# A half-block weight ring, reordered first casts and a moved lambda polynomial in a decoder layer

## What is computed

```
xn = rms_norm(x, mix_norm)
rnn_x, rnn_y, q, k_cmp, v_cmp, ..., merge_g = split(xn @ w_in)
y_rnn = gelu(rnn_y) * rg_lru(conv4(rnn_x), ..., rg_lambda)
y_nsa = native_sparse_attention(rms(q), compress_blocks(k_cmp, v_cmp; cmp_w1), ...)
y_sc  = sc_b * conv3(sc_c * sc_h)
x = x + (sum_b sigmoid(merge_g[b]) * (y_b @ P_b)) @ w_out
x = x + hierarchical_moe(rms_norm(x))      # 32 experts of 1024 x 256, top 1 group, top 2 in it
```

## Time and profile before

| | us |
|---|---|
| median of three runs | 462.19 |
| their lowest and highest | 461.26, 464.12 |
| profiled execution, span from first to last instruction | 459.2 |
| TensorE busy in it | 413.9 (90%) |
| VectorE busy | 217.9 (47%) |
| ScalarE busy | 173.8 (38%) |

### The profile page before, as it was taken

One profiled execution on the slowest core, in us unless ns is written; L12 is line 12 of the kernel. 1 busy time (PEld: TensorE's weight loads), 2 busy tenths in 40 slices (PEclk: granted clock), 3 DMA queues, 4 the chain that ended last, 5 costly groups with the idle time before them and its releaser, 6 DMA issues.

```text
span 459.2 us, 6635 instructions
## 1 busy us (share of the span) xinstructions
PE 413.9 (90%) x2701; PEld 292.7 (64%) x2701; DVE 217.9 (47%) x336; ACT 173.8 (38%) x270; POOL 40.0 (9%) x66
## 2 busy tenths in 40 slices
PE   6999999999999999999999999999929659299586
PEld 3889999999878787888888853535512413225122
DVE  5658988487799994564584650211100201002011
ACT  6558429873764565344256331110201101002001
POOL 8420490000000000000003100000000000000000
PEclk9999999999999999999999899999968959889799
DMA  8997893254552578897589989999999999999996
GB/s 291 348 260 257 327 387 105 100 184 184 183 183 93 185 250 298 286 410 266 183 364 359 387 355 425 423 421 420 428 424 421 422 422 425 424 414 414 400 394 220
DMA packets 43613, 146.27 MB, mean 319 GB/s; under 512 B 2908, under 2 KB 6097, under 8 KB 34242
## 3 DMA queue, kind: packets, MB, share of 16 engines
q1 hardware_dynamic: 42272, 143.50, 81.0%
q10 hardware_dynamic: 562, 1.84, 1.1%
q0 software_dynamic: 752, 0.55, 0.5%
HBM read 144.83 MB, written 1.05 MB: 318 GB/s over the span
## 4 chain that ended last, share of the span: by engine, by line
PE 62%; SPq 15%; DMA 14%; DVE 5%; ACT 2%; issue 2%; DVEq 0%
PE psum L1634 17%; DMA ring<-in_exp_w_down 10%; PE psum L1630 10%; PE psum L1877 7%; SPq L413 6%; PE psum L1927 5%; SPq L461 3%; PE psum L2145 3%; PE psum L2048 3%; DMA a_att<-in_exp_w_down 3%; SPq L429 3%; PE psum L1695 2%; SPq L418 2%; PE psum L2017 2%; PE psum L1769 1%
## 5 line engine op out<-in xcount | busy, mean ns | idle before, releaser
L1085 DVE TENSOR_TENSOR wl<-ring,wh 128x2048 fp32r<-128x2048 f32 (+1 forms) x38 | 85.1, 2245 | 36.5 <-ACT wh L750 35.8
L750 ACT CAST wh<-ring 128x2048 fp32r<-128x2048 f32 (+1 forms) x37 | 69.1, 1868 | 52.6 <-PE psum L1634 21.0
L1574 DVE COPY mix<-psum 128x512 f32<-128x512 f32 (+1 forms) x8 | 5.3, 658 | 115.7 <-PE psum L2145 110.0
L1634 PE MATMUL psum<-wh,x_parts 128*128 128x512 f32 (+1 forms) x256 | 58.1, 379 | 0.2 <-ACT a_att L877 0.2
L1634 PEld LDWEIGHTS psum<-wh,x_parts 128*128 128x128 f32 x256 | 46.0, 188 | 9.1 <-issue 0.4
L1035 ACT COPY mix<-psum 128x512 f32<-128x512 f32 x8 | 4.7, 586 | 103.5 <-PE psum L2145 100.4
L2048 PE MATMUL psum<-a_att,mix 128*32 128x512 f32 x96 | 25.6, 693 | 18.0 <-DMA a_rnn<-in_exp_w_up 17.0
L1630 PE MATMUL psum<-x_parts,wh 128*128 128x256 f32 x320 | 40.5, 284 | 0.0
L1630 PEld LDWEIGHTS psum<-x_parts,wh 128*128 128x128 f32 x320 | 39.1, 192 | 0.1
L2048 PE MATMUL psum<-odd,mix 128*32 128x512 f32 x192 | 24.2, 661 | 10.0 <-DMA odd<-in_exp_w_up 8.8
L2145 PE MATMUL psum<-ring,a_moe 128*32 128x512 f32 x152 | 27.6, 658 | 5.1 <-DMA ring<-in_exp_w_down 5.1
(11 more groups left out here) (319 smaller groups left out, 629.7 us busy)
## 6 DMA issues: line engine op xcount, KB each, us to landing
ring<-in_w_in SPq DMA_DIRECT2D x11, 2048.0 KB, 7.8
ring<-in_exp_w_down SPq DMA_DIRECT2D x19, 1024.0 KB, 15.8
odd<-in_exp_w_gate SPq DMA_DIRECT2D x12, 1024.0 KB, 14.8
odd<-in_exp_w_up SPq DMA_DIRECT2D x12, 1024.0 KB, 16.8
a_att<-in_exp_w_gate SPq DMA_DIRECT2D x8, 1024.0 KB, 14.9
a_att<-in_exp_w_up SPq DMA_DIRECT2D x8, 1024.0 KB, 16.9
mix<-in_exp_w_down SPq DMA_DIRECT2D x6, 1024.0 KB, 27.6
a_rnn<-in_exp_w_gate SPq DMA_DIRECT2D x4, 1024.0 KB, 21.4
```

The source lines that it names most:

```text
L750: a.copy(high, src).then_inc(hi_ready, 1)
L1085: signal(v.tensor_tensor(low, src, halves(m, wh)[1].bitcast(fp32), ALU.subtract), lo_ready, m + 1)
L1634: ins = t_.matmul(bank(name)[:, 0:n], xp[hf][:, k, i * P:(i + 1) * P], wv[:, k, :], start=start, stop=stop)
```

## The change

The ring has the same bytes, but the pieces now use only its upper half: three places of 2048 columns (1 MB), at column 6144. Piece m goes to place m mod 3. Each piece is loaded by its own DMA (piece 0 by two), and SP waits before piece m until `lo_ready` is m - 2, so until the low part of piece m - 3 is made. The lower half of the ring is free for other data: `cmp_w1` is loaded at once to columns 0 to 4095, right behind the first three pieces, and the same columns take `first_group(3)` as soon as the compression product is through. `down_half(0, 0)` goes to the columns behind, at once too. `odd_half(3, 0)` and `down_half(1, 0)` are issued behind pieces 3 and 4 instead of ahead of block sc. `even[3]` to `even[5]` are now the ring from the bottom up, and so the last three down halves change places. On ScalarE the two casts of q's piece 0 stand ahead of the upper halves of the input, and xT2 ahead of xT1. On VectorE the low part of piece 0 stands ahead of xT1 and xT3. The lambda chain stands between the low parts of pieces 4 and 5 instead of behind both.

```diff
-LOADS = (["q", "kva", "kvb", "rx", "cmp", "ry", "sb", "sc", "sh"]
+LOADS = (["q", "kva", "kvb", "rx", "ry", "sb", "sc", "sh"]
...
-        ring = sb("ring", [P, RING, SLOT])
+        ring = sb("ring", [P, 3 * SLOT])
+        HALF = SLOT // 2
+        PIECES_AT = 3 * SLOT - RING * HALF
+        cmp_weights = ring[:, 0:SLOT]
...
-                ring[:, 2, :], ring[:, 0, :], ring[:, 1, :]]
+                ring[:, 0:SLOT], ring[:, SLOT:2 * SLOT], ring[:, 2 * SLOT:]]
...
+        def piece_at(m):
+            return ring[:, PIECES_AT + (m % RING) * HALF:][:, 0:HALF]
...
+            def load_piece(m):
+
+                if m >= RING:
+                    sp.wait_ge(lo_ready, m - RING + 1)
+                name, hf = PIECES[m]
+                dst = halves(m, wh)[0]
+                if m == 0:
+                    for i in range(2):
+                        k = slice(2 * i, 2 * i + 2)
+                        sp.dma_start(dst[:, k], piece_source(name, hf)[:, k]).then_inc(q_quarter[i], 16)
+                else:
+                    sp.dma_start(dst, piece_source(name, hf)).then_inc(piece_full[m % RING], 16)
+
+            def load_cmp():
+                for kv in range(2):
+                    sp.dma_start(cmp_weights[:, kv * LP * P:(kv + 1) * LP * P].rearrange("p (l n) -> p l n", l=LP),
+                                 cmp_w1[0, kv].rearrange("(l p) n -> p l n", p=P)).then_inc(cmp_full, 16)
...
+            for m in range(len(PIECES)):
+
+                if m == PI["ry", 0] + 4:
+                    full(sp, "hidp")
+                    first_group(3)
+                if m == PI["ga2", 1]:
                     sp.wait_ge(yl_ready, 1)
                     down_half(1, 1, True)
-                if name == "gb1":
+                if m == PI["w2", 1]:
                     sp.wait_ge(y_sc_ready, 1)
                     first_group(2)
-                if name == "w1":
+                if m == PI["gb1", 1]:
                     full(sp, "o3")
                     first_group(0)
                     first_group(1)
 
-                if i >= RING:
-                    used(sp, LOADS[i - RING])
...
-            used(sp, "w1")
-            first_group(3)
-
-            sp.wait_ge(lo_ready, PI["wo0", 0] + 1)
-            down_half(0, 0)
+                load_piece(m)
+
+                if m == RING - 1:
+                    load_cmp()
+                if m == PI["kva", 1]:
+                    odd_half(3, 0)
+                if m == PI["kvb", 0]:
+                    down_half(1, 0, True)
+                if m == PI["kvb", 1]:
+                    down_half(0, 0)
+
             sp.wait_ge(merged_ready, 4)
             odd_half(3, 1)
+
             sp.wait_ge(lo_ready, PI["wo1", 0] + 1)
-            down_half(0, 2)
+            down_half(0, 3)
             sp.wait_ge(lo_used, ENDED.count(None))
             odd_half(0, 0)
             sp.wait_ge(lo_ready, PI["wo0", 1] + 1)
             down_half(0, 1)
             sp.wait_ge(lo_ready, PI["wo1", 1] + 1)
-            down_half(0, 3)
+            down_half(0, 2)
...
             x_high(0)
+            first_split(0)
+            x_high(2)
+            first_split(1)
             x_high(1)
-            x_high(2)
-            first_split(0)
             x_high(3)
-            first_split(1)
             done[0] = 1
             splits(3)
...
             x_scale(1, 1)
-            x_low(1, 2)
-            x_low(2, 3)
+            x_low(2, 2)
+            splits(1)
+            x_low(1, 3)
             x_low(3, 4)
             splits(4)
...
-            splits(6)
+            splits(5)
             dve.wait_ge(lam_exp, 1)
...
             chain(v.scalar_tensor_tensor(small[:, 48:52], acc, -4.0, small[:, 16:20], ALU.mult, ALU.add))
             signal(v.tensor_scalar(small[:, 52:56], small[:, 48:52], 2.0, None, ALU.mult), lru_scale, 1)
+            splits(6)
             for i, kk in enumerate((kvs, kvw)):
...
-            loaded(pe, "cmp")
+            pe.wait_ge(cmp_full, 32)
```

More of the change, by code:

```diff
@@ L81 @@
 BK["xT1"], BK["xT2"] = BK["xT2"], BK["xT1"]
-SPLIT = [n for n in LOADS if n != "cmp"]
-PIECES = [(n, hf) for n in SPLIT[:-2] for hf in range(2)] + [("wo0", 0), ("wo1", 0), ("wo0", 1), ("wo1", 1)]
+PIECES = [(n, hf) for n in LOADS[:-2] for hf in range(2)] + [("wo0", 0), ("wo1", 0), ("wo0", 1), ("wo1", 1)]
 PI = {p: i for i, p in enumerate(PIECES)}
@@ L89 @@
 WB = [f"w{b}" for b in BR]
-MADE = {n: (f"{n}_0", f"{n}_1") if n[0] == "g" else (f"{n}0", f"{n}1") for n in SPLIT if n not in WB}
+MADE = {n: (f"{n}_0", f"{n}_1") if n[0] == "g" else (f"{n}0", f"{n}1") for n in LOADS if n not in WB}
 MADE.update(wo0=("wo0", "wo2"), wo1=("wo1", "wo3"))
@@ L261, in trunk @@
         count_ps = h_ps[:, 0:E]
-        slot_full = [sem(f"slot_full{i}") for i in range(RING)]
+        piece_full = [sem(f"piece_full{i}") for i in range(RING)]
+        cmp_full = sem("cmp_full")
         even_full = [sem(f"even_full{i}") for i in range(NDOUBLE)]
@@ L311, in trunk, with piece_count @@
             "xg_act", "xg_dve", "o_act", "o_dve", "y_ready", "y_act", "stored"))
[L314 to L321, removed]
+        def piece_count(m):
+            return 16 * (m // RING + (m % RING > 0))
+        def piece_at(m):
+            return ring[:, PIECES_AT + (m % RING) * HALF:][:, 0:HALF]
         def place(j, odd_group):
@@ L342, in freed @@
             ins.then_inc(bank_free[BK[name]], 1)
[L344 to L349, removed]
         def high_free(eng, n):
@@ L392, in _, with piece_source @@
         def _(sp):
[L393 to L399 removed]
+            AT = dict(q=C_Q, kva=C_KC, kvb=C_KWN, rx=C_RX, ry=C_RY, sb=C_SB, sc=C_SC, sh=C_SH)
+            def piece_source(name, hf):
+                if name in WB:
+                    w = (w_rnn_out, w_nsa_out, w_sc_out)[int(name[1])]
+                    return w[0].rearrange("(k p) n -> p k n", p=P)[:, :, hf * CB:(hf + 1) * CB]
+                rows = slice(hf * KH, (hf + 1) * KH)
+                if name[0:2] == "wo":
+                    c0 = int(name[2]) * CB
+                    return w_out[0].rearrange("(k p) n -> p k n", p=P)[:, rows, c0:c0 + CB]
+                c0 = C_MG + int(name[2]) * D + (name[1] == "b") * CB if name[0] == "g" else AT[name]
+                return win_v[:, rows, c0:c0 + {"kvb": KVB}.get(name, CB)]
+            def load_piece(m):
[13 more added lines that the diff above has]
+                                 cmp_w1[0, kv].rearrange("(l p) n -> p l n", p=P)).then_inc(cmp_full, 16)
             def down_sem(e, odd_group):
```

54 lines of the change are left out of this document (4 added, 50 removed).

## The result

The changed kernel takes 466.90 us (median of 6 runs, 465.65 to 468.44) beside 462.13 us of the kernel before (6 runs, 461.26 to 464.12): ratio 1.0089, 95% interval 1.0061 to 1.0117. The forecast was 464.9 us with a range from 460.8 to 467.8. So it is slower by 0.9%: inside the range, inside the "within 1%" that the prediction thought likeliest, and 2.0 us above the point. The profiled executions have spans of 463.7 and 459.2 us. By the spans this is a loss of 4.5 us where 2.7 were forecast.

The account below looks back on a forecast made before the run. PE's trunk up to the first kpair_done, then the full load queue, bound the kernel. Span 459.2 + 2.7 for the late rx, start's gain spent, = 461.9, plus 3.0 around it: 464.9 us; range 460.8 to 467.8.

Parts of the forecast that it names:

- What bounds the kernel: PE's trunk up to the first kpair_done at 266.55 us, then the full load queue; nothing loaded before shortens the end.
- the 3 MB moved: first_group(3) and down_half(0, 0) leaving the stretch from 220 to 236 us: not waited for, worth 0.
- The start: PE's first product at 10.4 instead of 11.07 us through reordered casts: -0.67 us, as long as PE keeps it.
- Lambda: Sixteen operations, 3.2 us, moved into VectorE's idle hole between the low parts of pieces 4 and 5: 0.1 us gain.
- The queue at the start: Compression weights and expert blocks ahead of pieces 3 to 6 make PE begin rx at 42.9 instead of 40.23: +2.7 us.
- +2.7 us: PE's later begin of rx, 42.9 instead of 40.23, start's gain already spent, carried to kpair_done and the end.
- The waits of PE, one by one: PE waits about 1.3 us before piece 3, 0.7 at piece 5's low part, about 1.3 before rx.
- A: Queue at the start quick enough: piece 3 lands before 25, rx before 39, start's gain stays, 461.4 us; chance 0.26.
- B: Full stage really begins before 266.55, so 3.1 MB loaded early give 7.5 us: 454.7; chance 0.05.
- C: Compression weights' descriptors hold SP, piece 3 issued later than about 21.5 us, 2.4 us more: 467.3 us; chance 0.15.
- Half the lookahead: In the trunk, pieces issued once piece m - 3's low part is made: cost 0, hidden by casts waiting for hi_used.

Follow-up runs that it names:

- e9: e3 with first_group(3) and down_half(0, 0) issued where the kernel before had them, near 219 and 230 us; 461.16 us, ratio 0.9969.
- e7: e3 with first_group(3) and down_half(0, 0), 3 MB, both issued behind the last piece of the trunk; 464.88 us, ratio 1.0042.
- e3: Changed kernel with the compression weights behind piece 5 and the three early expert blocks behind piece 9; 461.66 us, ratio 0.9973.
- e4: Kernel before with only the new order of the first casts and the moved lambda chain; 461.12 us, ratio 0.9960.
- e11: e4 measured again: kernel before with only the new order of first casts and the moved lambda chain; 461.56 us, ratio 0.9983.
- e8: Changed kernel with the old order of the first casts on ScalarE and low parts on VectorE; 467.33 us, ratio 1.0116.
- e1: Changed kernel with the compression weights issued behind piece 3 instead of ahead of it; 467.09 us, ratio 1.0091.
- e5: Changed kernel with the compression weights' two DMAs reading 2 MB of w_in in 2 KB runs, for timing only; 464.68 us, ratio 1.0052.
- e10: e3 measured again with more rounds; 461.49 us, ratio 0.9981.
- e6: Changed kernel with sixteen extra products on TensorE ahead of piece 3, into a bank nobody reads; 468.39 us, ratio 1.0145.

## Why the prediction was right, and where it was off

**What bounds the kernel: right.** The end moved with the first `kpair_done` (+4.33 us, span +4.5), and the stage behind it ran at the same rate. The exact statement "nothing that is loaded before 266.55 shortens that sum" is true of the kernels before and after, where the queue has run dry, and e9 bears it out with the 3 MB moved. It hides a condition that e7 found: the full stage begins at the later of two times, `kpair_done` plus the latency, and the end of what is queued. Before, the queue's end stood 1.3 us behind the first issue (267.8 to 266.55), inside the latency of 5.1 us. In e7 it stood 8.2 us behind (274.7 to 266.5), group 2's first block landed at 277.0 instead of 271.6, and the kernel took 3.2 us more than e3. The 3.0 us around the span are in part luck: the profiled execution of before took 461.26 us, 2.1 over its span, and was the fastest of its six, as that of the changed kernel (465.74) is 1.2 under its median. This shifts both alike and leaves the difference.

**The start: right in where it begins, less sure in what it is worth.** First product at 9.99, forecast 10.4. The prediction took the first group to last as long as before. That held in the changed kernel (3.76 us for 3.78), but not in seven of the other executions, where the group began at half clock. The timed runs of e4 and e11 fit the -0.8 us forecast with lambda; their traces show no gain by rx. In the changed kernel the start is absorbed by the loads, as the prediction's sum had it (e8).

**Lambda: right.** From the start of rx to the transposes behind the compression product PE needs 58.16 - 44.51 = 13.65 us. Before it was 54.00 - 40.23 = 13.77: 0.1 us of gain.

**The queue at the start: the right mechanism, under-sized.** This is the step that made the 2 us. Forecast and measured landings: compression weights 23.9 and 23.1; piece 3 26.6 and 27.2; rx 41.0 and 42.1. PE on rx: 42.9 and 44.51. The term "+2.7 us" measured +4.28. Of the 1.6 missing, 1.1 is rx landing later: "Blocks of `w_in` go at 385 GB/s, 2.7 us a megabyte" was taken from a stretch without short runs, while piece 3 came 4.1 us behind the compression weights. The other 0.5 us is the sentence "rx is cast only at 41.0 + 1.9 = 42.9". Behind that cast ACT has the operations on kvb's results (L787, L788), and PE waits for the second of them. They stood in ACT's order of before too, but there the cast was made by 37.5, the second was over by 39.6, and PE came only at 40.23. In all eight executions in which rx's load ended PE's wait (after, e1, e5 to e10) PE began 2.41 or 2.42 us behind the landing.

**The waits of PE, one by one: partly wrong.** Forecast 1.3 us before piece 3, 0.7 at piece 5's low part and about 1.3 before rx; measured 2.41, none, 0.91, and 1.75 of half clock that was not in the forecast. e6 shows that how the loss is shared among them doesn't matter, only where rx lands. That is also why a sum that missed the half clock altogether came out near.

**Rivals.** A (the queue is quick enough) is out: rx landed 3 us later than A needs. e5 gives the size of what A was about: the runs of 512 bytes cost 2.7 us more over 2 MB than runs of 2 KB in `w_in`. The Trainium skill (DMA: Bandwidth & Descriptors, Specifications), by whose least transfer of 512 bytes both should go at line rate, is not borne out by 290 against 355 GB/s. B (early megabytes count) is out by e9 and e10, 461.16 and 461.49. C is half there: SP was held for 8.55 us, which the prediction had as a chance only. But the hold ended at 14.02, long before the 21.5 from which it decides, and it delayed piece 3's issue by 1.0 us at most (14.08 to 13.08 in e5). The time came close to C's 467.3, for another reason.

**Half the lookahead: right.** The ring of halves costs nothing that these runs can tell: e3, e9 and e10 have it and no wait for a piece in the trunk beyond 0.4 us at rx, and stand level with e11, which has the old ring.

**The best version.** e9 (the ring of halves, the new start and lambda, the compression weights behind piece 5, expert blocks where they fill idle stretches) is faster than both kernels by the times: 0.9969 (0.9949 to 0.9989) of the kernel before. e3, e4, e10 and e11 are no different from it. All five share the new start and lambda, and e4 and e11 have nothing else, so the gain of a microsecond or less comes with these two, and the new ring shows no worth either way.

**What can be told.** The prediction held that a measurement here can tell about 1% and that 2.7 us would read as no change. The intervals came out at some 0.3% to either side, and the loss of 0.9% is clear of them.

## What to carry to other kernels

Before more is loaded early, add up everything in the queue ahead of the next piece that the critical engine needs, and include small operations that stand behind the cast on the same engine. A wait that comes before a later, larger one costs nothing, so an account of lost time that adds up is no proof: remove one item and see whether the end moves. The loads that cost nothing here went where the queue had room (e3, e9), and the same loads cost 3 to 5 us at the start (changed kernel, e1) and in front of the stage that the queue bounds (e7). An earlier start of an engine is worth what is left of it a few steps on, so look there too, in more than one execution.

## What the runs showed of the hardware that was not expected

- The issue of a DMA can hold the queue's engine for long: the second load of the compression weights (1 MB in runs of 512 bytes) held SP 8.55 us when it was issued at 5.5 us, with more than 3 MB ahead of it that had not landed, and 1.5 us in the kernel before, on a queue with little in it. In runs of 2 KB it was 3.9 us (e5).
- Half clock can also reach into PE's first products: in e4 those up to about 12.3 us have a median of 628 ns, later ones 387 to 397, and the group of sixteen took 4.66 us instead of 3.76 (changed kernel). Whether it does so differs between executions of the same start (e3 3.76, e10 3.76, e9 4.15, e11 4.52). What decides isn't shown.
- Half clock follows some waits of PE in the middle of dense work and not others: after 2.41 us (changed kernel, 0.52 granted from 30 to 33.5 us) and after 2.23 (e5), but not after 2.16 and 2.21 (e6, e8); in e1 it came behind a wait of 1.78 (0.51 granted from 39.5 to 43 us). Each time it lasted some 3.5 us and made the group of products under it 1.5 to 1.75 us longer. What decides between the cases stays open. In e5 it fell behind rx's start and did cost: from there to the joint are 227.10 us instead of 225.7 to 226.4 in the others.
- Another stretch of half clock, some 3.4 us long and shortly before the joint, is in the kernels before and after, e4, e8 and e11 and not in e1 to e3, e5 to e7, e9 and e10. It makes about 0.6 us of that distance (226.20 to 226.37 with it, 225.65 to 225.77 without, e5 aside). No run here was made to find its cause.
